# Seven block products for eight in nine gate and up pairs of each feed-forward, set between the halves of a plain gate chunk

## The reference, cut to what matters

```
FFN_HIDDEN = 2816
y = rms_norm(x, g)
x = x + factor * ((silu(y @ w_gate) * (y @ w_up)) @ w_down)      # factor 1, 0.5, 0.5
```

## Time and profile before

| what | value |
|---|---|
| median of 3 runs | 2167.95 us (2167.79 to 2168.3) |
| the profiled execution | 2168.29 us, span 2166.5 us |
| mean granted clock of TensorE in it | 0.991 |
| PE, PEld busy | 2125.5 us, 1761.5 us |
| DVE, ACT, POOL busy | 1182.4, 894.9, 462.9 us |
| transfers | 222.91 MB, 103 GB/s |

### The profile page before, as it was taken

One profiled execution on the slowest core, in us unless ns is written; L12 is line 12 of the kernel. 1 busy time (PEld: TensorE's weight loads), 2 busy tenths in 40 slices (PEclk: granted clock), 3 DMA queues, 4 the chain that ended last, 5 costly groups with the idle time before them and its releaser, 6 DMA issues.

```text
span 2166.5 us, 28422 instructions
## 1 busy us (share of the span) xinstructions
PE 2125.5 (98%) x9960; PEld 1761.5 (81%) x9960; DVE 1182.4 (55%) x1981; ACT 894.9 (41%) x1542; POOL 462.9 (21%) x359
## 2 busy tenths in 40 slices
PE   8999999999999999999998999999999999999997
PEld 6788888888888888888886888888877888888886
DVE  5466764544442264443268777788768335444324
ACT  4345664422231152223133467676656324222212
POOL 2011344211110032220015601111165413111000
PEclk9999999999999999999999999999999999999999
DMA  4212235323333323333334422222263432333331
GB/s 170 78 54 68 87 125 174 97 89 96 97 97 116 96 80 97 97 97 107 97 101 138 125 69 69 84 74 75 87 213 137 180 97 88 97 97 97 111 96 65
DMA packets 66505, 222.91 MB, mean 103 GB/s; under 512 B 7312, under 2 KB 7568, under 8 KB 66032
## 3 DMA queue, kind: packets, MB, share of 16 engines
q1 hardware_dynamic: 51120, 182.08, 26.4%
q10 hardware_dynamic: 11712, 27.27, 3.4%
q0 software_dynamic: 3584, 12.39, 1.7%
HBM read 202.31 MB, written 18.87 MB: 102 GB/s over the span
## 4 chain that ended last, share of the span: by engine, by line
PE 86%; DVE 7%; POOL 2%; ACT 2%; issue 2%; DMA 1%; DVEq 0%; SPq 0%; POOLq 0%; ACTq 0%
PE bank L177 25%; PE bank L179 25%; PE bank L178 25%; PE bank L183 3%; PE bank L184 3%; POOL hid L543 2%; PE bank L1889 2%; DVE w_lo L151 1%; DMA w_raw<-stream 1%; DVE gn_r L2491 1%; DVE xn_lo L458 1%; PE bank L679 1%; PE bank L905 1%; POOL hid L1238 1%; DVE squares L226 0%
## 5 line engine op out<-in xcount | busy, mean ns | idle before, releaser
L151 DVE TENSOR_TENSOR w_lo<-w_raw,w_hi 128x1024 fp32r<-128x1024 f32 x337 | 458.6, 1364 | 529.4 <-ACT w_hi L146 527.0
L177 PE MATMUL bank<-xn_hi,w_hi 128*128 128x512 f32 x1624 | 647.2, 399 | 9.0 <-DVE w_lo L151 8.9
L179 PE MATMUL bank<-xn_hi,w_lo 128*128 128x512 f32 x1624 | 634.6, 391 | 0.0
L178 PE MATMUL bank<-xn_lo,w_hi 128*128 128x512 f32 x1624 | 634.3, 391 | 0.0
L146 ACT ACTIVATE w_hi<-w_raw 128x1024 fp32r<-128x1024 f32 x337 | 353.2, 1051 | 374.4 <-PE bank L179 251.2
L177 PEld LDWEIGHTS bank<-xn_hi,w_hi 128*128 128x128 f32 x1624 | 306.4, 189 | 72.6 <-DVE w_lo L151 9.7
L179 PEld LDWEIGHTS bank<-xn_hi,w_lo 128*128 128x128 f32 x1624 | 305.7, 188 | 64.9
L178 PEld LDWEIGHTS bank<-xn_lo,w_hi 128*128 128x128 f32 x1624 | 306.1, 188 | 62.4 <-issue 2.6
L549 POOL TENSOR_TENSOR h_lo<-hid,h_hi 128x512 f32 (+1 forms) x66 | 85.5, 1295 | 564.7 <-ACT h_hi L409 564.7
L177 PE MATMUL bank<-h_hi,w_hi 128*128 (+1 forms) x528 | 205.8, 390 | 0.0
L179 PE MATMUL bank<-h_hi,w_lo 128*128 (+1 forms) x528 | 205.4, 389 | 0.0
(11 more groups left out here) (414 smaller groups left out, 3121.6 us busy)
## 6 DMA issues: line engine op xcount, KB each, us to landing
w_raw<-stream SPq DMA_DIRECT2D x337, 512.0 KB, 3.6
spill_g<-gate_out ACTq DMA_DIRECT2D x16, 256.0 KB, 2.0
m_more<-spill_g POOLq DMA_DIRECT2D x3, 1024.0 KB, 11.8
x<-xt SPq DMA_DIRECT2D x4, 512.0 KB, 6.6
x<-xt ACTq DMA_DIRECT2D x1, 2048.0 KB, 9.1
spill_x<-x ACTq DMA_DIRECT2D x1, 2048.0 KB, 6.7
spill_ga<-ga_out ACTq DMA_DIRECT2D x8, 256.0 KB, 2.0
spill_rv_hi<-rv_hi_out ACTq DMA_DIRECT2D x8, 256.0 KB, 2.4
```

Of the source, the lines that this page charges most:

```text
L151: nc.vector.tensor_tensor(w_lo[:, slot, :], w_raw[:, slot % 2, :], w_hi[:, slot, :], ALU.subtract).then_inc(split_lo, 1)
L177: nc.tensor.matmul(to, a_hi, b_hi, start=start, stop=False, skip_group_check=True)
L178: nc.tensor.matmul(to, a_hi, b_lo, start=False, stop=False, skip_group_check=True)
L179: return nc.tensor.matmul(to, a_lo, b_hi, start=False, stop=stop, skip_group_check=True)
```

## The change

In the nine bodies of the loop the gate and up chunk of tile 2i are taken as one matrix of 256 x 1024, cut in 2 x 2 blocks: A11 and A12 are the gate's two halves along the inputs, A21 and A22 the up's. The input is cut likewise into four blocks, upper and lower half of the features by left and right half of the sequence (B11 to B22). The product of two such matrices takes eight block products; here it takes seven, each 4 x 3 matmuls of 256 columns, by Strassen's scheme in Winograd's form:
- S1 = A21 + A22, S2 = S1 - A11, S3 = A11 - A21, S4 = A12 - S2, made by POOL in each body in s_raw. For this POOL itself moves the two chunks a second time, by its own queue (raw_of), once DVE has made S4's low part of the body before (next_raw). ACT and DVE make high and low parts of each.
- T1 = B12 - B11, T2 = B22 - T1, T3 = B22 - B12, T4 = T2 - B21 (in the code with its sign changed), made once per feed-forward: ACT writes x times gain (scaled_x), POOL subtracts, ACT and DVE split.
- PE makes X = A11 B11 (bank 0), Y = A12 B21 (bank 1), A22 by T4 (bank 5), adds S2 T2 to bank 0, makes S1 T1 in bank 4, adds S3 T3 to bank 0 and S4 B22 to bank 4. Between them stand the two halves of the plain gate chunk of tile 2i + 1; its up chunk comes last.
- ACT copies bank 0 after X, bank 5, bank 0 after S2 T2 and bank 4 after S1 T1 into snaps, 256 columns each; DVE adds these to the banks, then norm_r and Silu come as before.
The hidden tiles are now kept as float32 (h), and ACT and POOL split them in the down stage, two chunks ahead, in four slots (down_hi, down_lo), in place of h_hi and h_lo. Semaphores of the merge stages are used again, with counts moved on. The stages around, the number of chunks in the stream and SP's program stay.

```diff
+                def block(to, a_hi, a_lo, b_hi, b_lo, start=True, stop=True):
+                    for k in range(HT):
+                        w = slice(k * P, (k + 1) * P)
+                        last = mm3(to, a_hi[:, w], a_lo[:, w], b_hi[:, k, :], b_lo[:, k, :], start and k == 0,
+                                   stop and k == HT - 1)
+                    return last
...
-                with pe.Fori(2, FT // 2) as i:
-                    for j in range(4):
-                        slot = ready(pe, first_in, j, i, N_IN)
-                        if j % 2 == 0:
-                            pe.wait_ge(s["product"], 2 * i + (b + j // 2 + 1))
-                        tile_chunk(slot, banks[j][:], xn_hi, xn_lo).then_inc(used, 1)
+                pe.wait_ge(c["lo"], c0["lo"] + 4)
+                with pe.Fori(FIRST_BODY, FT // 2) as i:
+                    gate = ready(pe, first_in, 0, i, N_IN)
+                    pe.wait_ge(s["product"], 2 * i + (b + 1))
+                    block(to_x, w_hi[:, gate, a1], w_lo[:, gate, a1], xn_hi[:, lower, left], xn_lo[:, lower, left],
+                          stop=False).then_inc(m["scaled"], 1)
+                    block(to_y, w_hi[:, gate, a2], w_lo[:, gate, a2], xn_hi[:, upper, left], xn_lo[:, upper, left]
+                          ).then_inc(used, 1)
+                    up = ready(pe, first_in, 1, i, N_IN)
+                    block(to_w, w_hi[:, up, a2], w_lo[:, up, a2], t_hi[:, C4], t_lo[:, C4]).then_inc(used, 1)
+
+                    plain = ready(pe, first_in, 2, i, N_IN)
+                    pe.wait_ge(s["product"], 2 * i + (b + 2))
+                    block(banks[2][:], w_hi[:, plain, a1], w_lo[:, plain, a1], xn_hi[:, lower, :], xn_lo[:, lower, :],
+                          stop=False)
+                    pe.wait_ge(c["lo"], part_made("lo", i, 1))
+                    pe.wait_ge(c["gate"], snapped(i, 1))
+                    block(to_x, s_hi[:, S2], s_lo[:, S2], t_hi[:, C2], t_lo[:, C2], False, False).then_inc(m["scaled"], 1)
+                    pe.wait_ge(c["lo"], part_made("lo", i, 2))
+                    block(to_z, s_hi[:, S1], s_lo[:, S1], t_hi[:, C1], t_lo[:, C1], stop=False).then_inc(m["scaled"], 1)
+                    block(banks[2][:], w_hi[:, plain, a2], w_lo[:, plain, a2], xn_hi[:, upper, :], xn_lo[:, upper, :],
+                          False).then_inc(used, 1)
+                    pe.wait_ge(c["lo"], part_made("lo", i, 4))
+                    pe.wait_ge(c["gate"], snapped(i, 3))
+                    block(to_x, s_hi[:, S3], s_lo[:, S3], t_hi[:, C3], t_lo[:, C3], False).then_inc(m["scaled"], 1)
+                    pe.wait_ge(c["gate"], snapped(i, 4))
+                    block(to_z, s_hi[:, S4], s_lo[:, S4], xn_hi[:, upper, right], xn_lo[:, upper, right], False
+                          ).then_inc(m["scaled"], 1)
+                    slot = ready(pe, first_in, 3, i, N_IN)
+                    tile_chunk(slot, banks[3][:], xn_hi, xn_lo).then_inc(used, 1)
...
# ACT, a body
+                    ahead(high_part, act, first_in, 0, i, N_IN)
+                    act.wait_ge(c["gated"], combined(i, 0))
+                    act.wait_ge(m["scaled"], multiplied(i, 1))
+                    snap(0, 0, i)
+                    s_high(S2, i)
+                    s_high(S1, i)
+                    finished(act, first_in, 1, i, N_IN)
+                    snap(1, 5, i)
+                    ahead(high_part, act, first_in, 1, i, N_IN)
+                    s_high(S3, i)
+                    s_high(S4, i)
+                    ahead(high_part, act, first_in, 2, i, N_IN)
+                    act.wait_ge(m["scaled"], multiplied(i, 2))
+                    snap(2, 0, i)
+                    act.wait_ge(m["scaled"], multiplied(i, 3))
+                    snap(3, 4, i)
+                    ahead(high_part, act, first_in, 3, i, N_IN)
+                    silu_of(1, 4 * i + (2 * b + 1))
+                    silu_of(0, 4 * i + (2 * b + 2))
...
# DVE, a body
+                    ahead(low_part, dve, first_in, 0, i, N_IN)
+                    s_low(S2, i)
+                    s_low(S1, i)
+                    dve.wait_ge(s["product"], 2 * i + (b + 2))
+                    finished(dve, first_in, 0, i, N_IN)
+                    dve.wait_ge(c["gate"], snapped(i, 1))
+                    joined(silu[0][:, 0:H], 1, 0)
+                    ahead(low_part, dve, first_in, 1, i, N_IN)
+                    s_low(S3, i)
+                    s_low(S4, i)
+                    ahead(low_part, dve, first_in, 2, i, N_IN)
+                    ahead(low_part, dve, first_in, 3, i, N_IN)
+                    finished(dve, first_in, 2, i, N_IN)
+                    normed(silu[1][:], 2, 0)
+                    dve.wait_ge(m["scaled"], multiplied(i, 5))
+                    dve.wait_ge(c["gate"], snapped(i, 4))
+                    joined(silu[0][:, H:S], 4, 2)
+                    dve.wait_ge(c["gated"], combined(i, 2))
+                    nc.vector.tensor_tensor(silu[0][:], silu[0][:], norm_r[:], ALU.mult).then_inc(s["scaled"], 1)
+                    joined(h_tile(i, 0, 0), 0, 1)
+                    joined(h_tile(i, 0, 1), 0, 3)
+                    dve.wait_ge(c["gated"], combined(i, 4))
+                    nc.vector.tensor_tensor(h_tile(i, 0), h_tile(i, 0), norm_r[:], ALU.mult).then_inc(s["scaled"], 1)
+                    gated(h_tile(i, 0), 0, 4 * i + (2 * b + 3), 2 * i + (b + 2))
+                    finished(dve, first_in, 3, i, N_IN)
+                    normed(h_tile(i, 1), 3, 0)
+                    gated(h_tile(i, 1), 1, 4 * i + (2 * b + 4), 2 * i + (b + 1))
...
# POOL
+                def sums(i):
+                    for g in range(2):
+                        pool.wait_ge(gates_in[g], 16 * i + (gates_loaded[g] + 16 * (1 - FIRST_BODY)))
+                    a11, a12, a21, a22 = (s_raw[:, g, half, :] for g in range(2) for half in range(2))
+                    nc.gpsimd.tensor_tensor(a22, a21, a22, ALU.add).then_inc(c["sum"], 1)
+                    nc.gpsimd.tensor_tensor(a21, a11, a21, ALU.subtract).then_inc(c["sum"], 1)
+                    pool.wait_ge(c["sum"], summed(i, 2))
+                    nc.gpsimd.tensor_tensor(a11, a22, a11, ALU.subtract).then_inc(c["sum"], 1)
+                    pool.wait_ge(c["sum"], summed(i, 3))
+                    nc.gpsimd.tensor_tensor(a12, a12, a11, ALU.subtract).then_inc(c["sum"], 1)
+                def next_raw(i):
+                    pool.wait_ge(c["lo"], part_made("lo", i, 4))
+                    raw_of(4 * i + (first_in + 4))
+                sums(FIRST_BODY)
+                if joint:
+                    nc.gpsimd.tensor_tensor(fin_r[:], x[:, 0, :], x[:, 0, :], ALU.mult).then_inc(f["added"], 1)
+                    with pool.Fori(FIRST_BODY, FIRST_BODY + KT - 1) as i:
+                        next_raw(i)
+                        square_added(i - 1, i - 1)
+                        sums(i + 1)
+                with pool.Fori(FIRST_BODY + (KT - 1 if joint else 0), FT // 2 - 1) as i:
+                    next_raw(i)
+                    sums(i + 1)
```

More of the change, by code:

```diff
@@ new lines, in t_high, with s_high, snap @@
+                def t_high(n, order):
+                    act.wait_ge(c["sum"], c0["sum"] + order + 1)
+                    nc.scalar.activation(t_hi[:, n], t_raw[:, n], ACT.Copy).then_inc(c["hi"], 1)
+                def s_high(n, i):
+                    act.wait_ge(c["sum"], summed(i))
+                    nc.scalar.activation(s_hi[:, n], s_of(n), ACT.Copy).then_inc(c["hi"], 1)
+                def snap(n, bank, i):
+                    nc.scalar.activation(snaps[:, n], banks[bank][:, 0:H], ACT.Copy).then_inc(c["gate"], 1)
@@ L412, in act_part @@
                 for t in range(4):
                     ahead(high_part, act, first_in, 4 + t)
-                    silus(t % 2, t // 2)
-                    highs(t % 2, t // 2)
-                with act.Fori(2, FT // 2) as i:
-                    for t in range(2):
-                        ahead(high_part, act, first_in, 2 * t, i, N_IN)
-                        silus(t, i)
-                        ahead(high_part, act, first_in, 2 * t + 1, i, N_IN)
-                        highs(t, i)
+                    if t == 0:
+                        for k in range(KT):
+                            nc.scalar.activation(scaled_x[:, k, :], x[:, k, :], ACT.Identity,
+                                                 scale=col[:, gain + k:gain + k + 1]).then_inc(c["gate"], 1)
@@ L422, in act_part, with down_high @@
+                def down_high(j, k):
+                    act.wait_ge(s["product"], k + (b + 3))
+                    nc.scalar.activation(down_hi[:, j % 4, :], h[:, bass.ds(k * S, S)], ACT.Copy).then_inc(s["hi"], 1)
+                act.wait_ge(m["scaled"], pb + 5 * BODIES)
+                for j in range(2):
+                    down_high(j, j)
                 if joint:
@@ L482, in dve_part, with joined @@
+                def joined(to, bank, n):
```

(18 more changed lines are left out.)

172 lines of the change are left out of this document (112 added, 60 removed).

## The result

The changed kernel takes 2173.15 us in the median of 7 runs (2168.09 to 2177.41), the kernel before 2167.95 (2166.40 to 2168.52, 7 runs): ratio 1.0024, 95% interval 1.0013 to 1.0036. The forecast was 2154.6 us with a range of 2146 to 2171. The profiled execution took 2171.12 us, span 2169.4.

The account below looks back on a forecast made before the run. The prediction took PE (TensorE) to bound the kernel. 20.2 us won in the loops, less 5.4 of in-loop waits and 1.5 at the starts, gave 13.3 us less: 2154.6 us as a median, 8 in 10 for 2146 to 2171.

Parts of the forecast that it names:

- Price of the products: PE in the loops: a body falls from 21.76 to 21.01 us, 20.2 us less over 27 bodies.
- The rule on weight loads: Loads overlap matmuls only across row groups; would cost a body 8 us; the prediction went by measured starts instead.
- In-loop wait: PE waiting in the loops for DVE's product, delayed by POOL's sums: 0.2 us a body, 5.4 over 27.
- the lock: POOL and DVE block each other by whole passes when both read two SBUF operands; up to 1.2 us per DVE pass.
- the tight place: End of the pair in each body: DVE's chain to the product ends at 19.1, PE wants it at 21.0; slack 1.9 us.
- Rivals C and D: Loops: POOL's loop sets the beat, 2190 or 2204 us, chance 0.11; or instructions are fetched again, 2203 us, chance 0.04.
- Once per feed-forward: Start of each feed-forward, T work ahead of the loop: 0.5 us, bounds 0 to 2; 1.5 us for three.
- No cost: Before chunk 6: tile 1's product comes between 435.7 and 436.8 us, PE wants it at 437.5.
- the T lows: Ahead of the loop: DVE's lows of 1.23 us follow POOL's sums, last at 442.5 to 449.6; loop starts at 448.4.
- The sum: Whole kernel: 20.2 - 5.4 - 1.5 = 13.3 us less, 2154.6 us as a median; chance 0.42 for 2150 to 2162.
- Rival B: Loops: the lock costs what was won, 0.5 to 0.75 us a body; 2163 to 2168 us, chance 0.13.

Follow-up runs that it names:

- e9: e4 with PE's first block product in the loops waiting for DVE's four joins of the body before, not for the tile pair's product; 2149.91 us, ratio 0.9916.
- e3: Changed kernel without the four T matrices and their making; block products read parts of x instead, so only loop time counts; 2151.82 us, ratio 0.9935.
- e4: Changed kernel with the loop one body later (24 bodies, not 27), T parts made beside plain tiles, chunks 6 and 7 in banks 6 and 7; 2156.24 us.
- e6: Changed kernel with POOL's four T sums cut to an eighth of their elements, ACT's and DVE's work kept in full size; 2156.45 us, ratio 0.9948.
- e2: Changed kernel with POOL making the first body's weight sums only after DVE's last T low part; 2167.11 us, ratio 0.9996.
- e7: e2 with chunks 6 and 7 of each feed-forward also in banks 6 and 7; 2164.72 us, ratio 0.9989.
- e11: e7 with all 27 bodies, T sums in half passes, and PE waiting for the joins as in e9; 2159.64 us, ratio 0.9968.
- e12: e11 with 9 dummy matmuls of 512 columns ahead of each loop, behind a wait for tile 1's product; 2158.53 us, ratio 0.9958.

## Why the prediction was wrong, by its steps

- **Price of the products** (21.01 us a body): right. 21.02 in all 21 undisturbed distances of e9, the matmuls 0.1196 apart, 0.03 for a change of width. The starts leave no room for a weight load that adds time to a narrow matmul. The rule on weight loads that the prediction takes from the Trainium skill (TensorE: Matmul & The Clock Gate) stands on that page under The mechanism; no body here shows the cost that it would give.
- **In-loop wait** (0.2 us a body, by the lock in the tight place): mechanism right, size about half in the changed kernel: 2.4 us over 27 bodies in the profiled execution (forecast 5.4), 0.13 a body in e3, 0.2 in e4, and nothing once PE does not wait for that product (e9). Rivals C and D did not come; the transfers took 6.5 us.
- **"Once per feed-forward ... I take 0.5 us, 0 to 2 as bounds"**: this is the step that failed. It measured 16.1 us of waits (5.7, 6.5 and 4.0) and 3.2 of lower clock behind them (of which 1.6 replaced a wait): 6.4 a feed-forward and not 0.5. Two sub-steps of it were wrong. "No cost" for tile 1's product between 435.7 and 436.8: it ended at 439.94, and that is 436.6, inside the bounds, plus 3.3 us in three passes held up by POOL. And the T lows: the text charged POOL 3.4 us a sum beside DVE, and DVE nothing beside POOL, though its own argument for the loops was that the two block each other, and whole passes at that. In the loops it priced the lock; at the start, with passes twice as long, it forgot the other side. e6 shows it with nothing else cut: short sums, 16 to 17 us.
- **The sum**: 20.0 won, 5.4 + 1.5 charged, 22.0 paid. Rival B named this lock as eating the gain, but put it in the loops at 0.5 to 0.75 us a body, and its end was the kernel before; none of the rivals sat at the start. The lower clock behind a wait stood in no term and no rival.

Still open: why the first feed-forward of the changed kernel kept its clock behind a wait of 3.1 us, while e2 and e7 had the lower one behind two of three waits of 2.2 to 2.6 us and e11 behind three of three of 1.9. And what makes the changed kernel's runs spread over 9 us, where those of the kernel before spread over 2 beside them and over 4 to 8 in the others. The runs point to the clock: its mean was 0.987 and 0.988 in the two slowest (2177.41 and 2175.08 us) and 0.990 or 0.991 in the rest. But only one run of them was profiled, and in which stages the others had it lower is not shown.

## What to carry to other kernels

When two engines exclude each other by whole passes, charge both queues with it, and most of all where one of them makes its longest passes; then ask what stands behind the held passes in the in-order queue. One-time work that feeds a loop wants its loop to start later: a plain body given up cost 0.74 us and hid some 6. A wait is best put on the last read of what it protects, not on the handiest signal behind it; that took 4.5 us off the feed-forwards (e9 against e4; 6 in the medians), where reordering the blocking work only moved the block. And a difference of 2 us between two kernels is worth a look at where in the trace it lies: between e7 and e2, and between e12 and e11, most of it lay in stages that both share.

## What the runs showed of the hardware that I had not expected

- A DVE pass with two SBUF operands of 128x1024 takes 1.22 us alone, 1.71 to 2.31 beside POOL passes of 512 elements, 2.83 beside those of 1024; the wait grows with the length of the other's pass.
- PE standing for 1.9 us was enough for the granted clock to be 0.57 and 0.65 in the 4 us behind, the lower level for most of it (17 narrow matmuls 0.213 us apart); behind waits of 1.1 us it stayed at 1.00. Not every such wait had it: behind one of 3.1 us and two of 2.3 in the changed kernel the matmuls kept their pace; behind its third wait of 2.3 us they did not. With dummy matmuls in the wait it stayed at 1.00 as well.
- Slowness of PE can be free: at the full clock (e12) it ran into waits of 0.5 and 0.3 us in the stretch where the lower one (e11) had none, and the changed kernel lost as much ahead of the loop in its first feed-forward (5.7 us, full clock) as in its third (5.6 us, 1.6 of them by the lower one).
